# MLP down projection by seven products of halves instead of eight, with weight low parts on VectorE and squares on ScalarE

## The reference, cut to what matters

```python
hn = rmsnorm(h, mlp_norm_g)                     # 512 x 1024
a = square(relu(hn @ w_up))                     # w_up 1024 x 4096
h = h + a @ w_down                              # w_down 4096 x 1024
out = rmsnorm(h, final_norm_g)
```

## Time and profile before

| What | us |
|---|---|
| median of 3 runs (1015.84 to 1016.77) | 1015.89 |
| the profiled execution's own time | 1016.66 |
| its span | 1014.9 |
| TensorE busy | 1004.7 |
| VectorE busy | 522.1 |
| ScalarE busy | 420.1 |
| GpSimd busy | 583.9 |

### The profile page before, as it was taken

One profiled execution on the slowest core, in us unless ns is written; L12 is line 12 of the kernel. 1 busy time (PEld: TensorE's weight loads), 2 busy tenths in 40 slices (PEclk: granted clock), 3 DMA queues, 4 the chain that ended last, 5 costly groups with the idle time before them and its releaser, 6 DMA issues.

```text
span 1014.9 us, 12887 instructions
## 1 busy us (share of the span) xinstructions
PE 1004.7 (99%) x4967; PEld 849.0 (84%) x4967; DVE 522.1 (51%) x879; ACT 420.1 (41%) x689; POOL 583.9 (58%) x724
## 2 busy tenths in 40 slices
PE   9999999999999999999999999999999999999997
PEld 7888788888888888888899977888888888888886
DVE  5781256665374743445679988865123213312324
ACT  4553355555562224443246685554222222222332
POOL 4555455664756874564658878456545545545470
PEclk9999999999999999999999999999999999999999
DMA  7323222112453125323223122322322342243132
GB/s 231 115 83 100 83 84 82 44 42 84 125 169 111 56 80 189 126 83 102 64 84 109 59 84 87 95 79 94 124 87 79 104 132 76 83 130 99 63 104 83
DMA packets 84829, 99.16 MB, mean 98 GB/s; under 512 B 3698, under 2 KB 69904, under 8 KB 84768
## 3 DMA queue, kind: packets, MB, share of 16 engines
q1 hardware_dynamic: 84464, 98.07, 30.1%
q10 hardware_dynamic: 304, 0.27, 0.1%
HBM read 96.23 MB, written 2.10 MB: 97 GB/s over the span
## 4 chain that ended last, share of the span: by engine, by line
PE 92%; DVE 5%; ACT 1%; issue 1%; DVEq 0%; ACTq 0%
PE ps L455 62%; PE ps L474 19%; PE ps L865 2%; PE ps L600 1%; PE ps L524 1%; PE ps L621 1%; PE ps L585 1%; PE ps L584 1%; PE ps L662 1%; PE ps L507 0%; DVE Hl L1399 0%; DVE tmp L1896 0%; PE ps L500 0%; DVE Al L2050 0%; PE ps L691 0%
## 5 line engine op out<-in xcount | busy, mean ns | idle before, releaser
L2159 POOL TENSOR_TENSOR wlo<-raw,whi 128x256 fp32r<-128x256 f32 x648 | 505.3, 812 | 326.0 <-ACT whi L873 325.9
L873 ACT ACTIVATE whi<-raw 128x1024 fp32r<-128x1024 f32 (+1 forms) x164 | 172.2, 1050 | 148.5 <-PE ps L474 91.0
L455 PE MATMUL ps<-Hh,whi 128*128 128x512 f32 x512 | 201.9, 394 | 0.7 <-DVE Hl L1399 0.7
L455 PE MATMUL ps<-Hl,whi 128*128 128x512 f32 x512 | 199.5, 390 | 0.0
L455 PE MATMUL ps<-Ah,whi 128*128 128x512 f32 (+1 forms) x576 | 196.5, 364 | 0.2 <-DVE Al L2050 0.2
L455 PE MATMUL ps<-Al,whi 128*128 128x512 f32 (+1 forms) x576 | 194.8, 361 | 0.0
L455 PE MATMUL ps<-Hh,wlo 128*128 128x512 f32 x512 | 129.3, 389 | 0.3 <-POOL wlo L2159 0.3
L455 PE MATMUL ps<-Ah,wlo 128*128 128x512 f32 (+1 forms) x576 | 124.4, 360 | 0.0
L455 PEld LDWEIGHTS ps<-Ah,whi 128*128 128x128 f32 x576 | 103.0, 188 | 16.9 <-DVE Al L2050 0.8
L455 PEld LDWEIGHTS ps<-Al,whi 128*128 128x128 f32 x576 | 103.0, 188 | 15.9
L455 PEld LDWEIGHTS ps<-Hh,whi 128*128 128x128 f32 x512 | 96.2, 188 | 20.8 <-DVE Hl L1399 1.4
(11 more groups left out here) (309 smaller groups left out, 1187.7 us busy)
## 6 DMA issues: line engine op xcount, KB each, us to landing
raw<-in_w_in SPq DMA_DIRECT2D x29, 1024.0 KB, 5.4
raw<-in_w_up SPq DMA_DIRECT2D x16, 1024.0 KB, 5.3
raw<-in_w_down SPq DMA_DIRECT2D x32, 512.0 KB, 3.3
raw<-in_w_in SPq DMA_DIRECT2D x14, 512.0 KB, 3.7
raw<-in_w_att_out SPq DMA_DIRECT2D x4, 1024.0 KB, 5.1
raw<-in_w_sg_out SPq DMA_DIRECT2D x4, 1024.0 KB, 5.1
raw<-in_w_o SPq DMA_DIRECT2D x4, 1024.0 KB, 5.0
Fm<-in_x SPq DMA_DIRECT2D x1, 2048.0 KB, 7.8
```

The costliest lines, as they stand in the source:

```text
L455: mm = e.matmul(ps[:, bk, 0:c1 - c0], of(j)[:, k % kk, 128 * g:128 * g + 128], x[:, k, c0:c1], start=(start and n == 0), stop=(stop and n ...
L873: return e.activation(out, src, ACT.Copy, scale=scale)
L2159: ins = e.tensor_tensor(w_lo(j)[:, *cut], raw_tile(j)[:, *cut], f(w_hi(j))[:, *cut], ALU.subtract)
```

## The change

The down projection of a part is cut in halves: activations X in two halves of 512 hidden features and two of 256 tokens, weights W in four quarters of 512 x 512, the result in four quarters of 256 x 512. Instead of eight products of such halves it forms seven, of sums of the halves, and gets the four results by adding these up. In the order of the list they are P11, P_7, P_5, P12, P_6, P_3, P_4. P11, P12 take halves as they are; P_7, P_5, P_6 and P_3 need a sum of activation halves; P_7, P_5, P_6 and P_4 need a sum of weight quarters.

- TensorE (`down`): a product is two tiles h of 12 matmuls: 2 row tiles x 2 slices of features x 3. In a tile both row tiles take the high weights first, then the low ones.
- P_3 and P_4 stay in banks 4 to 7 over all four parts. The others rotate over two pairs of banks, so P_5, P12 and P_6 need the bank that VectorE reads behind P11, P_7 and P_5, and the next part's up tiles those of P12 and P_6.
- SP loads `w_down` as quarters of 1 MB, in SBUF of their own, once each per part, when the last use of the quarter in the part before is through.
- VectorE forms the operand sums (`x_sums`), the weight sums (`w_sum`, a half of a quarter each), the low parts of the operands (`a_low`) and of all 14 down tiles (`w_low`), each one instruction of 1024 elements, and reads the banks (`out`). `act` becomes one instruction of 512, max(y, 0) times the factor.
- In part 3, `spread_sums` adds the collected products into the results (eight instructions of 1024, each waiting for the one before), between `act(3, 6)` and the first `w_low`; `last_out` then adds each product to two results.
- ScalarE casts weights and operands as before and squares the activations (`act_square`). There are five places for down tiles (cast j waits for the products of j - 5).
- GpSimd makes low parts of the up tiles alone in the MLP.
- The residuals are transposed two by two behind up tiles 3 to 6 of part 0.
- The end: P_4 runs row by row behind P_3, and the norm goes in the order rows 0, 1, 2, 3, with three more instructions of 1024 and four products with gamma ahead.

The diff's core (TensorE, then ScalarE, then VectorE, then SP):

```diff
+            def down(part, n):
+                xh, xl = x_slot(part, n)
+                kept = n in (P_3, P_4)
+                w.wait_ge("a_high", (part, n))
+                for h in range(2):
+                    j = down_tile(part, n, h)
+                    w.wait_ge("hi", j)
+                    ks = (2 * h, 2 * h + 1)
+                    for low in range(2):
+                        for r in range(2):
+                            if h == 0 and low == 0 and not (kept and part):
+                                w.wait_ge(*down_free(part, n, r))
+                            for k, x in ([(k, xh) for k in ks] if low else [(k, x) for x in (xh, xl) for k in ks]):
+                                if x is xl:
+                                    w.wait_ge("a_low", (part, n))
+                                if low:
+                                    w.wait_ge("w_low", j)
...
+            def down_free(part, n, r):
+                if n == P_4:
+                    return "residual_set", 7 - r
+                if n == P_3:
+                    return "drained", up_tile(0, r)
+                if n in (P11, P_7):
+                    return "drained", up_tile(part, (4 if n == P11 else 6) + r)
+                return "down_out", (part, {P_5: P11, P12: P_7, P_6: P_5}[n], r)
...
                     if part == 0 and n == 2:
                         mlp_sums()
-                    if part == 0 and n >= 3:
-                        residual(n - 3)
-                for h in range(2 if part < 3 else 1):
...
+                    if part == 0 and 3 <= n < 7:
+                        residual(2 * n - 6)
+                        residual(2 * n - 5)
+                for n in range(7 if part < 3 else 6):
+                    down(part, n)
...
+            def act_square(part, n):
+                w.wait_ge("drained", up_tile(part, n))
+                e.activation(X[:, n], X[:, n], ACT.Square).then_inc(*b.done("act_set", (part, n)))
+
+            for n in range(3, 8):
+                if n < 6:
+                    cast(up_tile(0, n) + 2)
+                if n < 7:
+                    residual(2 * n - 6)
+                    residual(2 * n - 5)
+                for i in {3: (0,), 4: (1, 2), 5: (3,), 6: (4,)}.get(n, ()):
+                    act_square(0, i)
+                if n in (5, 6):
+                    a_high(0, n - 5)
+            cast(down_tile(0, P11, 0))
+            act_square(0, 5)
+            cast(down_tile(0, P11, 1))
+            act_square(0, 6)
+            for h in range(2):
+                cast(down_tile(0, P_7, h))
+            for part in range(4):
+                if part:
+                    for n in range(8):
+                        cast(up_tile(part, n) + 4)
+                        if n:
+                            act_square(part, n - 1)
+                        if n in (4, 5):
+                            a_high(part, n - 4)
+                act_square(part, 7)
+                for i in range(14):
+                    j = down_tile(part, 0, 0) + i + 4
+                    if j < n_tiles:
+                        cast(j)
+                    for n in {1: (P_5,), 2: (P12,), 4: (P_6,), 7: (P_3,), 8: (P_4,)}.get(i, ()):
+                        a_high(part, n)
...
             def act(part, n):
...
-                scaled(y, UP_BANKS[min(part, 1)][n], RB, j)
-                w.wait_ge("drained", j)
-                e.scalar_tensor_tensor(y, y, 0.0, y, ALU.max, ALU.mult).then_inc(*b.done("act_set", (part, n)))
-                w.wait_ge("act_high", (part, n))
-                low(Hl[:, n], y, Hh[:, n]).then_inc(*b.done("act_low", (part, n)))
...
+                e.scalar_tensor_tensor(X[:, n], ps[:, up_bank(part, n), :], 0.0, RB, ALU.max, ALU.mult).then_inc(
+                    *b.done("drained", j))
...
+            def last_out(n):
+                for r in range(2):
...
+                    w.wait_ge("vector_step")
+                    e.tensor_tensor(y, y, bank, ALU.add).then_inc(*(signal if n == P12 else step()))
+                    if n == P11:
+                        e.tensor_copy(acc[0][:, r], bank).then_inc(*signal)
+                    elif n != P12:
+                        e.tensor_tensor(y2, y2, bank, ALU.subtract if n == P_7 else ALU.add).then_inc(*signal)
+
+            def spread_sums():
+                add(acc[3], acc[0], ALU.subtract)
+                add(y_half(0, 0), acc[0])
+                add(acc[2], acc[3])
+                add(y_half(0, 1), acc[2])
+                add(y_half(1, 1), acc[2])
+                add(y_half(1, 1), acc[1])
+                add(y_half(1, 0), acc[1], ALU.subtract)
+                add(y_half(1, 0), acc[3], ALU.subtract)
...
             for part in range(4):
+                send = last_out if part == 3 else lambda n, part=part: out(part, n)
+                for n in range(4):
                     act(part, n)
+                x_sums(part, P_7)
+                act(part, 4)
+                a_low(part, P11)
+                w_sum(part, P_7, 0)
+                w_sum(part, P_7, 1)
+                act(part, 5)
+                a_low(part, P_7)
+                w_sum(part, P_5, 0)
+                w_sum(part, P_5, 1)
+                act(part, 6)
+                if part == 3:
+                    spread_sums()
+                for i in range(4):
+                    w_low(part, i)
+                act(part, 7)
+                x_sums(part, P_5)
+                w_low(part, 4)
+                a_low(part, P_5)
+                w_sum(part, P_6, 0)
+                w_low(part, 5)
+                send(P11)
+                x_sums(part, P_6)
+                w_low(part, 6)
+                a_low(part, P12)
+                w_sum(part, P_6, 1)
+                send(P_7)
+                w_low(part, 7)
+                a_low(part, P_6)
+                w_low(part, 8)
+                x_sums(part, P_3)
+                send(P_5)
+                w_low(part, 9)
+                w_sum(part, P_4, 0)
+                a_low(part, P_3)
+                w_low(part, 10)
+                w_sum(part, P_4, 1)
+                w_low(part, 11)
+                w_low(part, 12)
+                a_low(part, P_4)
+                w_low(part, 13)
+                send(P12)
+                send(P_6)
...
+            w.wait_ge("down_out", (3, P_6, 1))
+            add(y_half(0, 1), acc[3])
+            w.wait_ge("final_g_in", 0)
+            for r in range(2):
+                times_g(r, 0, 512, "first_times", r)
+            e.tensor_tensor(y_half(1, 1), y_half(1, 1), acc[3], ALU.add).then_inc(*b.done("y22_set", 0))
+            add(y_half(1, 0), acc[3], ALU.subtract)
+            w.wait_ge("y22_set", 0)
+            for r in range(2, 4):
+                times_g(r, 512, 512, "first_times", r)
+            for r in range(2):
+                last_add(r, 0, down_bank(3, P_3, r), 512, 512)
+            for r in range(4):
+                first_mean(r)
+            for r in range(2):
+                last_mean(r, 0)
+            for r in range(2):
+                scale_left(r)
+            last_add(2, 0, 6, 0, 512)
+            last_mean(2, 0)
+            scale_left(2)
...
+            for part in range(4):
+                up = first_up + 4 * part
+                load_block(up)
+                load_block(up + 1)
+                if part == 0:
+                    w.wait_ge("conv_in_low", 1)
+                    load_quarter(0, 0, 0)
+                    load_quarter(0, 1, 0)
+                    w.wait_ge("conv_products", 1)
+                    load_quarter(0, 0, 1)
+                    load_quarter(0, 1, 1)
+                else:
...
+                    w.wait_ge(*low_ready(down_tile(part - 1, P_4, 1)))
+                    load_quarter(part, 0, 1)
+                load_block(up + 2)
+                load_block(up + 3)
```

More of the change, by code:

```diff
@@ L110, in weight_blocks @@
         cols("w_up_2", 0, 1024 * i, 4)
-        for h in range(2):
-            for k in range(4):
-                cols("w_down_2", 1024 * i + 256 * k, 512 * h, 1, 2, 1)
+        tiles.extend((None, (i, n, h)) for n in range(7) for h in range(2))
     return blocks, tiles
@@ L127 @@
 TAPS = 22
+P11, P_7, P_5, P12, P_6, P_3, P_4 = range(7)
 def build(nc, t):
@@ L875, in cast @@
             def cast(j):
-                blk = tiles[j][0]
-                w.wait_ge(f"raw_in{blk % 2}", blk)
-                if j >= n_kept:
-                    w.wait_ge("products", (up_tile(3, 7), 0))
-                elif j >= 3:
-                    kk = blocks[tiles[j - 3][0]][3]
-                    w.wait_ge("products", (j - 3, {8: 0, 4: 1, 2: 3}[kk]))
+                blk, i = tiles[j]
+                if blk is not None:
+                    w.wait_ge(f"raw_in{blk % 2}", blk)
+                else:
+                    part, n, h = i
+                    if n in (P11, P12, P_3):
+                        w.wait_ge(f"quarter{int(n != P11)}{int(n == P_3)}_in", part)
+                    else:
```

(17 more changed lines are left out.)

378 lines of the change are left out of this document (235 added, 143 removed).

## The result

The changed kernel takes 1021.56 us (median of 4, 1021.11 to 1021.74) against 1016.25 for the kernel before (4 runs): ratio 1.0051, 95% interval 1.0034 to 1.0069. It is slower by 5.3 us; the forecast was 4.9. The profiled execution took 1021.11 us at a span of 1019.3.

What follows compares the result with a forecast made beforehand. TensorE bounds the kernel before; VectorE's list would decide part 3. TensorE gives back 21.8 us, part 0 takes 3.5 and the end 23.4, so about 5 us slower: 1020.8 us, range 1013 to 1031.

Steps and rivals of the forecast that it cites:

- part 0's down stretch beyond 38.08: Part 0: TensorE waits for banks and P11's first low part, together 3.5 us, bounds 0 and 7.
- T3: Start of P11 in part 3, forecast at 952.55 us, against 965.65 for its counterpart before.
- T: Time in us counted from where TensorE starts P11 of the part.
- the 23.4 us: From up tile 6 of part 3 to the end, 23.4 us of VectorE's making are added.
- Part 3's wait for P11's bank: In part 3 TensorE waits 3.3 + 0.3 us for P11's bank.
- Rival 4: TensorE's clock falls behind the waits, costing 2 to 3 us in part 0: 1023 us; chance 0.06.
- The tail: After part 3's last bank read, VectorE's additions, gamma products, means and scaling take 17.4 us, to T = 64.1.
- The lead of the casts: Middle parts: five weight places let casts run four tiles ahead, 10.9 us against 1.06 + 2.82; no wait.
- Rival 2: Full VectorE pitch everywhere, 1.26 and 0.73 us, slowing parts 0 to 3: 1032 us; chance 0.10.
- The rule: VectorE's next instruction starts only once the pipeline is empty, so all pitches would be 1.26 and 0.73 us.
- Rival 1: VectorE is not the bound; 1024s behind act 6 pitch under about 1.0 us: 1004 us; chance 0.12.
- Rival 3: No net change: part 0's waits do not come, the tail overlaps by a microsecond: 1016 us; chance 0.12.

Runs made afterwards that it cites:

- the second profile: The changed kernel run once more without further change, beside the filler runs: 1021.13 us, ratio 1.0044 to the kernel before.
- The two moves: Against the changed kernel: part 3's sums ahead of act 0 (1011.91 us); part 0's ScalarE squares and high parts ahead of residual copies (1016.84 us); both, 1008.00 us.
- the first profile: The profiled execution of the changed kernel at its first timing: 1021.11 us, with a median of 1021.56 us.
- the ScalarE move: Against the changed kernel, part 0's squares of tiles 3 to 5 and high parts of P11 and P_7 go ahead of residual copies: 1016.84 us, ratio 1.0005.
- the filler: Changed kernel plus ten matmuls into an unused bank ahead of TensorE's wait for P11's bank in part 0: 1020.90 us, ratio 1.0043.
- the two fillers together: Changed kernel plus ten unused matmuls in part 0 and twenty ahead of P11's first low part in part 3: 1020.86 us, ratio 1.0041.
- the three places: Changed kernel with three places for weight tiles instead of five, cast j waiting for products of j - 3: 1055.85 us, single execution.
- GpSimd's tail: Both moves, plus GpSimd making two last additions and two gamma products behind the last bank read: 1008.88 us, ratio 0.9925.

## Why the prediction was right

Against its own steps:

| Step | predicted | measured |
|---|---|---|
| matmuls taken out | 96, 38.08 us a down stretch | 38.08 |
| independent 1024, dependent 1024 | 1.14, 1.26 | 1.13, 1.26 |
| first bank reads in parts 1 and 2 end | 8.9, 14.7, 20.5 | 9.0, 14.7, 20.4 |
| P11 of part 0 starts | 704.25 | 703.13; 704.13 in the second profile |
| part 0's down stretch beyond 38.08 | 3.5 | 4.7 (the clock's share in it); 3.8 in the second profile |
| P11 of part 3 starts (T3) | 952.55 | 947.41 + 5.44 = 952.85 |
| eight sums, to the next start | 10.08 | 958.12 - 948.04 = 10.08 |
| wait at P11's first low part | 4.7 | 4.74 |
| last bank read ends | T = 46.7 | 999.26, T = 46.4 |
| TensorE ends | T = 49.3 | 1002.56, T = 49.7 |
| scaling ends (ScalarE's share) | T = 64.1 | 1015.59 + 0.61 = 1016.20, T = 63.4 |
| span | 1019.8 | 1019.3 |

The mechanism is the one forecast. The gain of 5.44 us a part on TensorE is exact wherever it does not wait; it is spent by the list of a VectorE which is busy for only 63% of the span, but has its free time in the wrong place. The two moves show the parts: 4.3 to 4.7 us for part 0 and 9.2 to 9.7 for the sums, 13.1 to 13.6 together. What remains of the 23.4 us that the prediction put down to the end of part 3, some 14 us, was not separated by a run. By the rows it is mostly VectorE's own work, the double bank reads in `last_out` and 17 us of tail, and in part its waits for ScalarE ahead of P_5; handing a part of the tail to GpSimd brought nothing in this form.

What was off, in small terms that cancelled:
- T3 was met within 0.3 us in the first profile by two misses that cancel, which is luck: P11 of part 0 starts 1.1 us sooner than forecast and the stretch loses 1.2 us more, mostly the clock's price. In the second profile both terms are within 0.3 us. The agreement of 4.9 with 5.3 us is not luck in the main, since the large terms were met one by one; how close the two numbers come is.
- Part 3's wait for P11's bank was forecast as 3.3 + 0.3 and is 1.07, mostly because the matmuls before it ran at the lower clock: with the clock at 1.00 there it is 2.98. P_5 still starts at T = 18.9 (18.9 by the prediction's steps): VectorE's list decided, TensorE's speed did not.
- Rival 4, the clock, came true in half of its claim. It falls, in some executions also in part 0, but costs 1.0 us in part 0 (2 to 3 forecast, from some ten matmuls for which it had no row) and nothing in part 3. The Trainium skill, TensorE: Matmul & The Clock Gate, section "HAM oscillation", describes gaps that bring the array back to half rate; here the 4.7 us gap does so in each of the two profiles of the changed kernel, the 2.4 us gap in one of them.
- The tail was 16.9 us instead of 17.4.
- The lead of the casts was held against 2.82 us for a low part, GpSimd's price; in the down tiles VectorE makes it, in 1.22. Nothing hung on it.
- Rival 2 (full pitch everywhere) is refuted by the row at 973.83, which starts 0.08 us before the end of the one before it, and by the last bank read at T = 46.4. The rule as the prediction took it from the Trainium skill, VectorE: DVE Perf Modes, section "The DRAIN you can't avoid", does not hold for this list; the same section adds "A next op that is not held starts earlier", which the prediction left out and with which this row agrees. Rival 1 fails by the same rows: the pitch is 1.13 us, not under 1.0. Rival 3 needed part 0 without waits: that is what the ScalarE move made, 1016.84.

The experiments' own misses are the filler (1.9 expected, at most 0.7 seen), for the expectation took one execution's clock for all and left out the small waits that slower matmuls hide; the two fillers together, where the clock was to stay at 1.00; the three places (12 to 20 expected, 34 seen); part 0's wait with the squares back on VectorE; and GpSimd's tail (2 us gain expected).

## What to carry to other kernels

When work goes from a full engine to a half empty one, walk down the receiving engine's list in order and hold each due time against it: an instruction that could run any time in the 10 idle microseconds before costs its full length behind the last act. Here the placement of eight additions, three squares and two high parts was worth some 13.4 us, nearly two thirds of what the seven products saved, and turned a loss of 0.5% into a gain of 0.8%.

## What was not expected of the hardware

- Whether TensorE's clock falls behind a wait of 2.4 us differs between executions of the same kernel: eight matmuls behind it took 3.14 us in one profile and 2.08 in the other.
- The start of the kernel differs too. The 22 matmuls of 128 columns at the start took 4.22 us in the profile with the fall and 5.07 in the one without. What follows stands later in the second by 0.85 us right behind them, 1.4 at 611 and 1.0 from 672 to the wait in part 0. Of the five profiles that have this wait (1.9 to 2.4 us, the three weight places left aside), the two with the short start (4.22, 4.33) are those in which the clock fell; the three with the long one (4.99, 5.07, 5.07) kept it. No run shows whether the two belong together.

```profile
1.19 4.22 PE L597 MATMUL ps<-ones 128*128 128x128 f32 x22 [1.19 <-DVE ones L1567]
```

```profile
1.20 5.07 PE L597 MATMUL ps<-ones 128*128 128x128 f32 x22 [1.20 <-DVE ones L1567]
```

- A VectorE instruction of 512 elements in SBUF took up to 2.83 us beside GpSimd instructions of 1024 (0.69 alone), whereas beside GpSimd's 256s a 1024 took 1.69 at most. The Trainium skill, SBUF — State Buffer, section "Who interferes with whom", calls the ports that VectorE shares with GpSimd an exclusive lock and has a VectorE instruction with two SBUF inputs contend with a GpSimd instruction that reads SBUF. The traces agree, and in these two cases the price goes with the length of GpSimd's instruction.
